# Up projections in matmul pairs that leave their output turned, and last chunks of the output and down projections by token tile

## What is computed

```
def first_block(x, ...):
    h = rms_norm(x, pre_mix_norm)
    ... h @ w_in, differential and sparse attention -> mix
    x = x + rms_norm(mix @ w_out, post_mix_norm)
    h = rms_norm(x, pre_ffn_norm)
    u = causal_dwconv(h @ w_up, conv_w, conv_b)          # width 3, along the tokens
    gate, up = jnp.split(u, 2, axis=-1)                  # 2 x 5632 features
    x = x + rms_norm((gelu(gate) * up) @ w_down, post_ffn_norm)

def second_block(x, ...):
    h = rmsnorm(x, norm_pre_mix)
    ... h @ hgrn_w_in, gated recurrence in both directions -> o
    x = x + rmsnorm(o @ hgrn_w_out, norm_post_mix)
    h = rmsnorm(x, norm_pre_ffn)
    up = dwconv3(h @ ffn_w_in, ffn_w_conv)               # width 3, centred
    gate, val = jnp.split(up, 2, axis=-1)
    x = x + rmsnorm((silu(gate) * val) @ ffn_w_out, norm_post_ffn)
```

## Time and profile before

| What | us |
|---|---|
| Median of 3 runs (lowest, highest) | 2574.31 (2570.81, 2574.83) |
| The profiled execution | 2571.86 |
| Its span, first to last instruction | 2569.8 |
| PE busy | 2520.8 |
| DVE busy | 1629.2 |
| ACT busy | 1343.4 |
| GpSimd (POOL) busy | 194.3 |
| Up projection, 20 half groups of one phase | 453.40 |

### The profile page before, as it was taken

One profiled execution on the slowest core, in us unless ns is written; L12 is line 12 of the kernel. 1 busy time (PEld: TensorE's weight loads), 2 busy tenths in 40 slices (PEclk: granted clock), 3 DMA queues, 4 the chain that ended last, 5 costly groups with the idle time before them and its releaser, 6 DMA issues.

```text
span 2569.8 us, 38318 instructions
## 1 busy us (share of the span) xinstructions
PE 2520.8 (98%) x14284; PEld 2121.5 (83%) x14284; DVE 1629.2 (63%) x1874; ACT 1343.4 (52%) x1749; POOL 194.3 (8%) x93
## 2 busy tenths in 40 slices
PE   8999999999999999999999999999999999999997
PEld 8999877788888888887888888888788888888886
DVE  5565674676666765445485868775666676765444
ACT  5454564656556554444645454554656556554442
POOL 1000000021121211000000000000021121211000
PEclk9999999999999999999999999999999999999999
DMA  7865345556666666665665555546556666666654
GB/s 223 254 205 150 114 127 183 157 179 188 181 189 188 181 187 204 187 198 175 190 176 166 172 159 176 158 148 197 157 179 187 188 188 186 179 185 207 190 188 146
DMA packets 241788, 462.07 MB, mean 180 GB/s; under 512 B 14344, under 2 KB 23361, under 8 KB 241169
## 3 DMA queue, kind: packets, MB, share of 16 engines
q1 hardware_dynamic: 240001, 453.44, 58.2%
q0 software_dynamic: 1568, 7.10, 0.9%
q10 hardware_dynamic: 112, 0.03, 0.0%
HBM read 458.40 MB, written 2.12 MB: 179 GB/s over the span
## 4 chain that ended last, share of the span: by engine, by line
PE 98%; DVE 1%; ACT 1%; issue 0%; DMA 0%; SPq 0%; DVEq 0%; ACTq 0%
PE acc L229 26%; PE acc L231 25%; PE acc L230 25%; PE acc L783 3%; PE acc L786 2%; PE acc L785 2%; PE tp L472 2%; PE acc L1010 1%; PE acc L1011 1%; PE acc L1012 1%; PE tp L275 1%; PE tp L1490 1%; PE acc L791 1%; PE acc L793 1%; PE acc L792 1%; PE tp L1518 1%
## 5 line engine op out<-in xcount | busy, mean ns | idle before, releaser
L216 DVE TENSOR_TENSOR wlo<-raw,whi 128x1024 fp32r<-128x1024 f32 x856 | 1150.9, 1358 | 790.7 <-ACT whi L211 788.3
L211 ACT ACTIVATE whi<-raw 128x1024 fp32r<-128x1024 f32 x856 | 903.6, 1060 | 1009.6 <-PE acc L231 844.0
L229 PE MATMUL acc<-whi,ahi 128*128 128x512 f32 x2176 | 857.5, 394 | 0.0
L231 PE MATMUL acc<-whi,alo 128*128 128x512 f32 x2176 | 847.9, 390 | 0.0
L230 PE MATMUL acc<-wlo,ahi 128*128 128x512 f32 x2176 | 847.0, 389 | 0.0
L231 PEld LDWEIGHTS acc<-whi,alo 128*128 128x128 f32 x2176 | 408.5, 188 | 86.2
L229 PEld LDWEIGHTS acc<-whi,ahi 128*128 128x128 f32 x2176 | 408.9, 188 | 83.2 <-issue 0.7
L230 PEld LDWEIGHTS acc<-wlo,ahi 128*128 128x128 f32 x2176 | 409.1, 188 | 81.7
L229 PE MATMUL acc<-whi,hhi 128*128 128x512 f32 x704 | 274.1, 389 | 0.0
L231 PE MATMUL acc<-whi,hlo 128*128 128x512 f32 x704 | 273.9, 389 | 0.0
L230 PE MATMUL acc<-wlo,hhi 128*128 128x512 f32 x704 | 273.9, 389 | 0.0
(11 more groups left out here) (237 smaller groups left out, 1930.5 us busy)
## 6 DMA issues: line engine op xcount, KB each, us to landing
raw<-in_w_up_dram SPq DMA_DIRECT2D x176, 512.0 KB, 4.1
raw<-in_ffn_w_in_dram SPq DMA_DIRECT2D x176, 512.0 KB, 4.0
raw<-in_hgrn_w_in_dram SPq DMA_DIRECT2D x160, 512.0 KB, 3.7
raw<-in_w_in_dram SPq DMA_DIRECT2D x88, 512.0 KB, 3.7
raw<-in_w_down_dram SPq DMA_DIRECT2D x88, 512.0 KB, 3.7
raw<-in_ffn_w_out_dram SPq DMA_DIRECT2D x88, 512.0 KB, 4.2
raw<-in_w_out_dram SPq DMA_DIRECT2D x32, 512.0 KB, 3.6
raw<-in_hgrn_w_out_dram SPq DMA_DIRECT2D x32, 512.0 KB, 3.9
```

Of the source, the lines that this page charges most:

```text
L211: act.activation(whi[:, s, :], raw[:, s, :], ACT.Copy).then_inc(hi_done, 1)
L216: dve.tensor_tensor(wlo[:, s, :], raw[:, s, :], whi[:, s, :].bitcast(F32), ALU.subtract).then_inc(lo_done, 1)
L229: pe.matmul(out[:, t, :], xh, whi[:, s, c], start=(kt == 0), stop=False)
L231: mm = pe.matmul(out[:, t, :], xl, whi[:, s, c], start=False, stop=(kt == nk - 1))
```

## The change

It has two parts.

In the up projections `products_turned` takes the place of `products`: 128×128 weights are stationary and the tokens stream, so the output has tokens on the free axis. `ahi` and `alo` now lie in one tensor `ahl`, and one matmul streams both (512 columns) past whi, the next streams ahi alone (256 columns) past wlo, into the first half of the same bank. The bank's two halves are added later: ACT copies the second half of each bank to `ut` (`low_part`), DVE adds the first (`evacuate`) and multiplies by 1/rms along the tokens (`scaled`, with a row `uprow` that one extra PE product per phase spreads over the partitions). A half group takes four banks: the gate half `acc[0]` and `acc[1]`, the other half `tp[0]` and `tp[1]`. `turn` and `utok` are gone; centre and convolution read `ut`. The splits of the first chunks of the down projection run further ahead (`TAIL_HI` 7, `TAIL_LO` 8).

In out1, down1, out2 and down2 the last four chunks are held in the ring together and run for token tile 0 first, then for token tile 1 (`last_products`). Square, root, reciprocal, ybuf and the additions of the last group go by token tile, with the sums of the three earlier groups reduced ahead (`rest_dve`), and the square is taken from `acc` rather than after ybuf. Transposes of quarters 0 and 1 go by token tile (`pre_pe_by_token`). The output leaves in five stores: all of token tile 0, then four quarters of token tile 1.

```diff
+        def part_banks(half, j):
+            return acc[j] if half == 0 else tp[j][:, :, :].rearrange("p (n k) t -> p n (k t)", n=NT)
+
+        def products_turned(pe, n, s, half, k0, ready=None, row=None):
+            pe.wait_ge(lo_done, n + 1)
+            for k in range(CK):
+                kt = k0 + k
+                if ready:
+                    pe.wait_ge(sem("pre_lo"), lo_ready(ready, kt))
+                for ct in range(4):
+                    c, o = slice(k * GC + ct * P, k * GC + (ct + 1) * P), part_banks(half, ct // 2)
+                    if row and k == 0 and ct == 3:
+                        pe.wait_ge(row, NT + 2)
+                    pe.matmul(o[:, ct % 2, :].rearrange("p (a t) -> p a t", a=2), whi[:, s, c], ahl[:, :, kt, :],
+                              start=(kt == 0), stop=False, skip_group_check=True)
+                    mm = pe.matmul(o[:, ct % 2, 0:S], wlo[:, s, c], ahi[:, kt, :], start=False, stop=(kt == KT - 1),
+                                   skip_group_check=True)
+            mm.then_inc(chunk_used, 1)
...
+        def last_products(pe, ph, k, n, xhi, xlo, kts):
+            out = acc[(gb[ph] + NG - 1) % 2]
+            for t in range(NT):
+                for j in range(RING):
+                    if t == 0:
+                        pe.wait_ge(lo_done, n + j + 1)
+                    s = (n + j) % RING
+                    for kk in range(CK):
+                        kt, c = kts[j] + kk, slice(kk * GC, (kk + 1) * GC)
+                        xh, xl = xhi[:, kt, t * P:(t + 1) * P], xlo[:, kt, t * P:(t + 1) * P]
+                        pe.matmul(out[:, t, :], xh, whi[:, s, c], start=False, stop=False)
+                        pe.matmul(out[:, t, :], xh, wlo[:, s, c], start=False, stop=False)
+                        mm = pe.matmul(out[:, t, :], xl, whi[:, s, c], start=False, stop=(j == RING - 1 and kk == CK - 1))
+                    if t:
+                        mm.then_inc(chunk_used, 1)
+                if t == 0:
+                    mm.then_inc(sem("token0"), 1)
...
+        def last_dve(dve, ph, k, gain_row, nxt):
+            add = add_rows(dve, ph, k)
+            unroot_dve(dve, ph, k, 0)
+            add(0, 0)
+            last_y(dve, ph, k, 0, gain_row)
+            s_lo(dve, nxt, 0, 0, 0)
+            add(1, 0)
+            s_lo(dve, nxt, 0, 0, 1)
+            unroot_dve(dve, ph, k, 1)
+            add(0, 1)
+            last_y(dve, ph, k, 1, gain_row)
+            add(1, 1)
...
         def up_pe(pe, ph, src_ready):
-            def turn(i, half):
-                pe.wait_ge(group_free, gb[ph] + half + 1 + i * 2)
-                for k in range(4):
-                    for t in range(NT):
-                        mm = pe.transpose(tp[half][:, k, t * P:(t + 1) * P], utok[half][:, t, k * P:(k + 1) * P],
-                                          ident[:, :])
-                mm.then_inc(sem(f"{ph}_uturned{half}"), 1)
             def body(i, first):
                 for c in range(BODY):
-                    if c % CPG == 0:
+                    if first and c == 0:
+                        pe.wait_ge(group_free, gb[ph])
+                    elif c % CPG == 0 and not first:
                         group(pe, gb[ph] + c // CPG + i * 2)
                     if first:
                         lead_pe(pe, ph, c, x, src_ready)
-                    products(pe, cb[ph] + c + i * BODY, c % RING, acc[(gb[ph] + c // CPG) % 2], ahi, alo,
-                             CK * (c % CPG), KT, ph if first and c < CPG else None)
-                    if c == 1 and not first:
-                        turn(i - 1, 1)
-                    if c == CPG + 1:
-                        turn(i, 0)
+                    products_turned(pe, cb[ph] + c + i * BODY, c % RING, c // CPG, CK * (c % CPG),
+                                    ph if first and c < CPG else None, sem(f"{ph}_row") if first and c == CPG else None)
+                    if first and c == CPG - 1:
+                        pe.wait_ge(sem(f"{ph}_row"), NT)
+                        pe.wait_ge(sem("ones"), 2)
+                        pe.matmul(tp[1][:, 2, :], upones[:, :], cvu[:, 0, :], start=True, stop=True)\
+                          .then_inc(sem(f"{ph}_row"), 1)
...
+            def evacuate(i, half):
+                dve.wait_ge(sem(f"{ph}_low"), i * 4 + (2 * half + 2))
+                for j in range(2):
+                    o = ut[half][:, 2 * j:2 * j + 2, :]
+                    m = dve.tensor_tensor(o, part_banks(half, j)[:, :, 0:S], o, ALU.add)
+                m.then_inc(group_free, 1)
+
+            def scaled(i, half):
+                dve.wait_ge(group_free, gb[ph] + half + 1 + i * 2)
+                dve.tensor_tensor(ut[half][:, :, :], ut[half][:, :, :], bcast(uprow[:, :], 1, 4), ALU.mult)\
+                   .then_inc(sem(f"{ph}_ut"), 1)
```

More of the change, by code:

```diff
@@ L88, in bass_two_blocks @@
         with ExitStack() as r:
-            utok = [sb(f"utok{j}", [P, NT, GC], where=r) for j in range(2)]
+            ut = [sb(f"ut{j}", [P, 4, S], where=r) for j in range(2)]
             cvg = sb("cvg", [P, 4, S], where=r)
@@ new lines, in last_act @@
+        def last_act(act, ph, k, t, end):
+            a, other = acc[(gb[ph] + NG - 1) % 2], acc[(gb[ph] + NG) % 2]
+            if t == 0:
+                act.wait_ge(sem("token0"), k + 1)
+            else:
+                act.wait_ge(chunk_used, end)
+            act.activation(other[:, t, :], a[:, t, :], ACT.Square, accum_out=psq[:, k, t, NG - 1:NG])\
+               .then_inc(sem("last_sq"), 1)
+            act.wait_ge(sem("last_sq"), NT * k + t + 1)
+            act.wait_ge(sem("rest"), 2 * k + 2)
+            act.activation(prs[:, k, t:t + 1], psq[:, k, t, NG - 1:NG], ACT.Sqrt, scale=1.0 / D,
+                           bias=rest[:, k, t:t + 1]).then_inc(sem("post_root"), 1)
@@ L348, in body, with back_pe @@
+        def back_pe(pe, ph, k, nch, ready):
+            pe.wait_ge(ready, FG)
+            for i in range(2):
                 for c in range(2 * nch):
@@ L382, in back_group_act, with back_act @@
             m.then_inc(group_free, 1)
-        def back_act(act, ph, k, nch, first_too=False, last=False):
-            def body(i, first, ahead=LEAD):
-                for c in range(LEAD, 2 * nch + ahead):
-                    if first:
-                        lead_act(act, ph, c, None)
+        def back_act(act, ph, k, nch, nxt):
+            for i in range(2):
+                for c in range(LEAD if i else TAIL_HI, 2 * nch + (0 if i else LEAD)):
                     s_hi(act, ph, i, 2 * nch, c)
@@ L437, in add_rows, with add @@
+                if not i:
+                    back_group_dve(dve, ph, i, 1, nch, gain_row)
+            if nxt:
+                last_dve(dve, ph, k, gain_row, nxt)
+            else:
+                for t in range(NT):
+                    unroot_dve(dve, ph, k, t)
+                    add_rows(dve, ph, k)(0, t)
+                    last_y(dve, ph, k, t, gain_row)
+                    for q in range(1, NG):
+                        add_rows(dve, ph, k)(q, t)
         def add_rows(dve, ph, k):
-            def add(q):
+            def add(q, t):
@@ L1014, in m1_pe @@
                 between(N1 + n)
+            last_products(pe, "out1", 0, N1 + len(LAID1) - RING, ahi, alo, [CK * PR1[q] for g, q in LAID1[-RING:]])
         def m1_act(act):
@@ L1540, in m2_pe @@
                 between(n)
-            for n in range(len(LAID2)):
+            for n in range(len(LAID2) - RING):
                 if n == 0:
@@ L1555, in m2_pe @@
                 between(N2 + n)
+            last_products(pe, "out2", 2, cb["out2"] + len(LAID2) - RING, ahi, alo, [CK * c for g, c in LAID2[-RING:]])
         LAID2 = ([(g, c) for g in range(2) for c in range(6)] + [(g, c) for g in range(2) for c in range(6, 8)]
@@ L1849, in m2_dve @@
                 between(n)
-            for n in range(len(LAID2) + LEAD):
+            for n in range(len(LAID2)):
                 if n in (3, 4, 5, 6):
@@ L1856, in m2_dve @@
                     out2_pre_dve(dve, n - 6)
[L1857 to L1860 removed]
+                s_lo(dve, "out2", 0, 0, n)
                 between(N2 + n)
@@ L1928, in _ @@
             up_act(act, "up1", 0, sem("out1_x"), 8)
-            back_act(act, "down1", 1, DCH)
+            back_act(act, "down1", 1, DCH, "in2")
             m2_act(act)
             up_act(act, "up2", 1, sem("out2_x"), 8)
-            back_act(act, "down2", 3, DCH, last=True)
+            back_act(act, "down2", 3, DCH, None)
         @block.vector
@@ L1938, in _ @@
             up_dve(dve, "up1", 0, add_rows(dve, "out1", 0))
-            back_dve(dve, "down1", 1, DCH, gbd)
+            back_dve(dve, "down1", 1, DCH, gbd, "in2")
             m2_dve(dve)
             up_dve(dve, "up2", 1, add_rows(dve, "out2", 2))
-            back_dve(dve, "down2", 3, DCH, gbd, last=True)
-            for q in range(4):
-                add_rows(dve, "down2", 3)(q)
+            back_dve(dve, "down2", 3, DCH, gbd, None)
```

255 lines of the change are left out of this document (142 added, 113 removed).

## The result

The changed kernel takes **2579.55 us** (median of 17 runs, 2578.39 to 2581.68); the kernel before, run beside it, 2574.16 us (16 of its 17 runs lie between 2570.81 and 2575.04; one took 4252.52 and doesn't move the median). The ratio is 1.0024 [1.0017, 1.0031]: **0.24% slower**. The forecast was 2536.5 us, 1.5% faster, with a range of 2528 to 2555; the time lies 24.5 us above its upper end. The profiled execution took 2578.8 us with a span of 2576.8 us and a mean granted clock of 0.997 (before: 2569.8 us of span, 0.993), so the clock isn't what was lost.

The account below looks back on a forecast made before the run. PE was taken as the bound, busy 98% of the span. 18.9 − 38.2 − 4.8 + 1.0 − 2.8 − 2.3 − 4.3 − 5.1 = −37.6 us gave 2536.5 us, range 2528 to 2555.

Parts of the forecast that it names:

- the 13.3 ns: All matmuls on PE: fixed cost beside the columns, whatever the width, giving 0.2267 us at 512 columns, 0.1200 at 256.
- is seen twice: Up projections: starts 0.12 and 0.23 us apart in the earlier trace show no weight load exposed when widths alternate.
- +18.9: Up projections: 32 more matmuls in each of 44 half groups, 22.19 us for 21.76, cost 18.9 us.
- (a): Up projections: the next 512-column matmul's weight load can't hide under the 256-column one; +208 us, some 2745 us; 5%.
- (b): Up phases: DVE or ACT falls behind; half a microsecond each half group would be +22, 2558 us; 8%.
- (c): Seams give back little, clock down in each and store late: 8.7 in place of 14.5 us, 2542.5 us; 20%.
- the seams: Stops between phases: −2.8 us at out1→up1, −2.3 at out2→up2, −4.3 at down1→in2, −5.1 at the end of down2.
- (d): Up projections: the fixed cost isn't paid for the added narrow matmuls; 18.9 us less, 2518 us; 4%.
- (e): Whole kernel: nothing changes within 0.2%, gains eaten by a loss of like size; 2%.
- The turns: Up projections: 42 turns of 8 transposes between products go, 0.91 us each, −38.2 us.
- up→down gap: End of each up phase: the last turn's 2.4 us wait goes and down products follow at once; two phases, −4.8 us.
- 18.9 − 38.2 − 4.8 + 1.0: Up projections: added matmuls, turns removed, last turn's gap removed in two phases, and the product spreading 1/rms along tokens.

Follow-up runs that it names:

- e5: The changed kernel with 192 unused bytes ahead of ybuf, putting whi a multiple of 256 bytes from ahl and hhi; 2552.03 us, ratio to before 0.992.
- e10: e5 with ahi and alo 32 bytes further on in the up phases only; 2534.65 us, ratio to before 0.9849.
- m2: Matmuls alone, no kernel: wide, narrow, paired and grouped four and four, at several operand distances; a pair takes 353.5 ns at 0 bytes, 346.9 at 96.
- e7: The changed kernel with the up projections of the kernel before, TAIL_HI and TAIL_LO 3, and 224 bytes ahead of ybuf; 2553.55 us, ratio to before 0.9925.
- m1: Matmuls alone, no kernel: 24 at each of 33 operand distances, 0 to 1024 bytes, 512 then 256 columns; 226.65 ns for 512 at multiples of 256.
- e11: e10 with PE's wait for group_free moved behind the 16 transposes; 2532.66 us, ratio to before 0.9837.
- e8: e5 with four 512-column matmuls and then four of 256 columns in place of pair after pair; 2547.22 us, ratio to before 0.9896.
- e9: e8 with PE's wait for group_free moved behind the 16 transposes; 2540.73 us, ratio to before 0.9872.
- e2: The kernel before with an unused tensor of 64 bytes ahead of ybuf; 2626.0 us, ratio to before 1.0204.

## Why the prediction was wrong, step by step

**The sum with what was measured.** Forecast −37.6 us. The place of the tensors, after against e5: +27.5. The pair's price, e5 against e10: +17.4. Together +7.3; measured 2579.55 − 2574.16 = +5.4. The 1.9 us left are of the size of the terms' own errors; e10, with both prices back at those of the forecast, takes 2534.65 us where 2536.5 were forecast. Two terms of some 45 us therefore account for the whole miss, each shown by an experiment that changes only where tensors lie.

**The step that failed first** is one that the prediction doesn't have. It prices what the change removes, adds and moves, and takes it that all other matmuls stay at 0.2267 us. The list of new tensors was in the diff, and 4992 wide matmuls in phases outside the up projections read tensors that lie behind them. That cost 27.5 us. Nothing in the trace of before could have told me the price, as its 512-column products have but one distance (modulo 256); what it could have told is that such a price might exist, since it doesn't say what the 13.3 ns are.

**The step that failed second** is "a matmul costs its columns plus a fixed 13.3 ns, whatever its width", and with it the sentence that no weight load's coming out "is seen twice". The earlier trace rows are two distances at a resolution of 10 ns, and I used their sum to 0.1 ns. Nor is their narrow matmul the pair's: the forms of L842 in the earlier trace rows, 128*30 and 128*60, are loads of 30 and 60 columns, listed with 106 and 131 ns, where both loads of a pair have 128 columns and 188 ns. Alternating at an aligned distance the pair costs 353.1 ns, 236.2 + 116.9: the wide one is 9.5 ns dearer than among its like and the narrow one 2.8 cheaper, too little to be seen in a timeline of hundredths. The term "+18.9" was +37 at that distance (2816 × 6.4 ns = 18.0 more). At 224 bytes off, e10, the number of the forecast is met to the nanosecond, 346.67 for 346.7. That is luck, as the reason given for it was wrong.

**The rivals.** (a), weight loads in the open, had the sign but not the size: the pair grew by 6.4 ns, not by 74, and less than the 13.4 ns from which it was to decide. By itself that would have left the kernel some 20 us faster. A whole load in the open is refuted. Whether a few nanoseconds of one are what the pair pays isn't known: moving the narrow one's weights alone takes them away (m2). (b) is refuted, as DVE is busy 15.7 us of each 22.6 (I had put 17.9 of 22.19) and no product in an up projection waits for it. (c) is refuted: e7 has 20.2 us for the seams. (d) doesn't hold, as the narrow matmul of a pair costs 116.9 to 119.6 ns for 106.7 of columns, nor does (e) as to its reason, though "gains eaten by a loss of like size" is what happened.

**The rule weighed.** The Trainium skill (TensorE: Matmul & The Clock Gate, "Back-to-back issue gap") has columns plus about 2.5 ns as the gap of isolated matmuls, and says itself that a stream in which each matmul has its load doesn't follow it, which the prediction left out. Here the smallest excess over the columns in an unmixed stream was 226.65 − 213.3 = 13.3 ns at 512 columns and 117.3 − 106.7 = 10.6 ns at 256 (m1), so it isn't the same at both widths either. The same page of the Trainium skill ("Step-by-step: what each phase is for") says that TensorE has two independent read ports, and that loading the next tile's weights takes no read bandwidth from the running matmul. The runs show something that this doesn't lead one to expect: where the two operands lie relative to each other changes a matmul by up to 7 ns, with no other engine at work (m1). Whether and where the two reads meet, no run here shows.

**What was right.** The turns and the up→down gap are gone, with no wait in their place. The seams: T + 5.76, 4.36, 7.05 and a tail of 7.49 for 5.7, 4.8, 5.7 to 7 and 8, the early transposes held by `group_free` (removing the wait brings T + 4.29 in e11), and the table load moved ahead. Their sum was put at 14.5 us. e7 measures 20.2, but it lacks `group_free`'s wait, which the two seams have in the full change (worth 1.0 to 3.3 us each, by e10 to e11 and e8 to e9). The up→down gap is not in it: e7 keeps the lone turn there, with 2.59 us between starts as in the kernel before (2.60). The first part is worth 20.9 us by e7 against e11, for 18.9 − 38.2 − 4.8 + 1.0 = −23.1.

**What stays open.** Why 256 bytes: the mechanism is inside the chip and was only bracketed. Why a pair whose two weights move together is cheapest at 96 and 224 bytes, why moving one of them alone does as much, and why grouped wide matmuls stay at 233.6. In which seams the clock falls: of two with a like stop of 2.7 us, out1→up1 kept it in the changed kernel and lost it in e10. And the last 2 us of the first part.

## What to carry to other kernels

When a diff adds or removes a tensor, look at what lies behind it, and hold the distance between the two operands of the hot matmuls in place, with a pad if need be; a byte count is part of the change. When phases that the change doesn't touch are slower, compare the mean distance of starts there first, before any theory on the part that it does touch. A price read from two starts at a hundredth of a microsecond isn't a price for 2816 pairs: take it from a long stretch of the same mixture, or keep a term of some nanoseconds times their number in the range.

## What the hardware showed that wasn't expected

- A 512-column fp32r matmul with a weight load each costs 226.65 ns where its two operands in SBUF lie a multiple of 256 bytes apart, 229.35 ns at 192 bytes, and 233.1 to 233.9 ns at the other multiples of 32 (m1). In the kernel before, 64 bytes cost 53 us of 2573 (e2).
- A 256-column one goes the other way: 119.6 ns at the multiple, 117.3 to 118.4 at the others but 160 bytes, which has 120.2 (m1).
- Alternating 512 and 256 columns costs 353.5 ns at the multiple and 346.8 to 346.9 where both weights lie 96 or 224 bytes off, but also 347 where only the narrow one's lie 32 to 160 bytes off (m2); 32 bytes on one tensor were worth 17.4 us (e5, e10).
- Reading the 512 columns as two runs 16 KB apart costs nothing (11.04 us for 48 either way, m2).
